# A streaming-encoder block on one core: q, the probabilities and the attention output turned by VectorE and GpSimd, none by TensorE

## The reference

```python
x = x + 0.5 * swiglu(rms_norm(x, norm_ffn1_w), ffn1_w_gate, ffn1_w_up, ffn1_w_down)      # width 5632
p = rms_norm(x, norm_mix_w) @ w_in                                                        # width 5376
# group A: 16 query heads of 64 over 2 key heads, chunks of 64 tokens; a chunk sees itself and the one before
logits = einsum('bnqhgd,bnkhd->bnhgqk', qc, kb) * 64 ** -0.5      # -inf where there is no chunk before
probs = softmax(concatenate([logits, sink], axis=-1))[..., :-1]
attn_out = einsum('bnhgqk,bnkhd->bnqhgd', probs, vb)
# group B: retention, 4 heads of 256: rotary(q), rotary(k), decay, group norm, swish gate
x = x + concatenate([attn_out, ret_out]) @ w_out
x = x + 0.5 * swiglu(rms_norm(x, norm_ffn2_w), ffn2_w_gate, ffn2_w_up, ffn2_w_down)
out = rms_norm(x, norm_final_w)
```

## Time and profile before

| | |
|---|---|
| median of 3 runs | 1823.14 us (1823.1 to 1823.24) |
| profiled execution | 1823.17 us, its span 1821.4 us |
| TensorE | 1807.5 us busy, 99% |
| VectorE | 1183.8 us busy, 65% |
| ScalarE | 823.5 us busy, 45% |
| GpSimd | 63.6 us busy, 3% |
| DMA, mean rate | 190 GB/s |

### The profile page before, as it was taken

How to read it: one execution, slowest core, us unless ns; L and a number is a source line. 1 busy time by engine, 2 the same in 40 slices (tenths; PEclk the granted TensorE clock), 3 DMA queues, 4 the chain that set the end, 5 groups by cost and what they waited for, 6 DMA issues and landing times.

```text
span 1821.4 us, 22695 instructions
## 1 busy us (share of the span) xinstructions
PE 1807.5 (99%) x8314; PEld 1495.8 (82%) x8314; DVE 1183.8 (65%) x1399; ACT 823.5 (45%) x986; POOL 63.6 (3%) x59
## 2 busy tenths in 40 slices
PE   9999999999999999999999999999999999999998
PEld 6888888888888888888888888888888888888886
DVE  5666676676676667544466665676676666667666
ACT  6434444443443445455555455444443443444444
POOL 0000000000000000100045000000000000000000
PEclk9999999999999999999999999999999999999999
DMA  9565565655556555555545456556556556555562
GB/s 371 194 199 185 197 194 187 199 189 191 201 185 196 195 186 187 182 167 179 163 160 185 139 176 208 194 186 203 187 191 201 185 195 197 186 199 191 189 204 93
DMA packets 175235, 346.64 MB, mean 190 GB/s; under 512 B 5984, under 2 KB 8416, under 8 KB 175072
## 3 DMA queue, kind: packets, MB, share of 16 engines
q1 hardware_dynamic: 174768, 345.61, 57.3%
q10 hardware_dynamic: 432, 0.55, 0.1%
HBM read 344.04 MB, written 2.10 MB: 190 GB/s over the span
## 4 chain that ended last, share of the span: by engine, by line
PE 98%; DVE 1%; DMA 1%; issue 0%; ACT 0%; SPq 0%; POOLq 0%; POOL 0%; DVEq 0%
PE ps L328 32%; PE ps L330 32%; PE ps L329 32%; PE ps L355 1%; DMA raw<-in_g 1%; DVE w_lo L850 0%; PE ps L475 0%; PE ps L563 0%; PE ps L574 0%; PE ps L488 0%; ACT w_hi L638 0%; PE ps L444 0%; PE ps L442 0%; PE ps L443 0%; DVE x L914 0%
## 5 line engine op out<-in xcount | busy, mean ns | idle before, releaser
L850 DVE TENSOR_TENSOR w_lo<-raw,w_hi 128x1024 fp32r<-128x1024 f32 x648 | 806.0, 1245 | 603.6 <-ACT w_hi L638 602.5
L638 ACT ACTIVATE w_hi<-raw 128x1024 fp32r<-128x1024 f32 x648 | 687.0, 1061 | 966.9 <-PE ps L330 957.1
L328 PE MATMUL ps<-w_hi,xT_hi 128*128 128x512 f32 (+1 forms) x1816 | 706.7, 389 | 1.7 <-DVE w_lo L850 1.1
L329 PE MATMUL ps<-w_lo,xT_hi 128*128 128x512 f32 (+1 forms) x1816 | 703.4, 387 | 0.0
L330 PE MATMUL ps<-w_hi,xT_lo 128*128 128x512 f32 (+1 forms) x1816 | 703.4, 387 | 0.0
L328 PEld LDWEIGHTS ps<-w_hi,xT_hi 128*128 128x128 f32 x1816 | 341.0, 188 | 72.5 <-DVE w_lo L850 1.6
L330 PEld LDWEIGHTS ps<-w_hi,xT_lo 128*128 128x128 f32 x1816 | 341.0, 188 | 70.1
L329 PEld LDWEIGHTS ps<-w_lo,xT_hi 128*128 128x128 f32 x1816 | 341.0, 188 | 68.7
L328 PE MATMUL ps<-w_hi,hT_hi 128*128 128x512 f32 x640 | 249.1, 389 | 0.0
L330 PE MATMUL ps<-w_hi,hT_lo 128*128 128x512 f32 x640 | 249.0, 389 | 0.0
L329 PE MATMUL ps<-w_lo,hT_hi 128*128 128x512 f32 x640 | 249.0, 389 | 0.0
(11 more groups left out here) (110 smaller groups left out, 499.2 us busy)
## 6 DMA issues: line engine op xcount, KB each, us to landing
raw<-in_u SPq DMA_DIRECT2D x88, 1024.0 KB, 5.1
raw<-in_d SPq DMA_DIRECT2D x88, 1024.0 KB, 4.9
raw<-in_g SPq DMA_DIRECT2D x87, 1024.0 KB, 5.1
raw<-in_w_in SPq DMA_DIRECT2D x40, 1024.0 KB, 4.9
raw<-in_w_out SPq DMA_DIRECT2D x16, 1024.0 KB, 5.0
x<-in_x SPq DMA_DIRECT2D x4, 512.0 KB, 12.6
raw<-in_w_in SPq DMA_DIRECT2D x4, 512.0 KB, 3.6
out<-proj SPq DMA_DIRECT2D x8, 256.0 KB, 2.4
```

The source lines that it names most:

```text
L328: pe.matmul(out, xh, wh, start=first and j == 0, stop=False)
L329: pe.matmul(out, xh, wl, start=False, stop=False)
L638: act.activation(dst, raw[:, s, (k % 2) * HALF:(k % 2 + 1) * HALF], ACT.Copy).then_inc(hi_ready, 1)
L850: dve.tensor_tensor(w_lo[:, k % LEAD, :, :].rearrange(flat), raw[:, k // 2, (k % 2) * HALF:(k % 2 + 1) * HALF], f32(w_hi[:, k % LEAD, :, : ...
```

## The change

No block of q, probabilities or attention output goes through TensorE any more. VectorE turns a whole tile at once, but each 32 by 32 square where it stands (`dve.transpose` from SBUF to SBUF), and GpSimd copies the squares to the partitions where they belong: 8 copies for q, 16 for the probabilities, 16 for the attention output, each of 32 partitions. The results lie in `qT`, `probsT` and `attT_raw` (in `qT_full`) in SBUF. `q_in` and `att` become the two halves of one tile, `stage_tile`; the turned probabilities are put over both. `weigh` moves from behind half 10 to behind half 11, the division from VectorE's position 10 to 12, `attT_hi` and `attT_lo` from 13 to 15. GpSimd's loop over quads is written out. The core of the diff, with the waits:

```diff
@@ tensor
             def weigh(quad):
-                pe.wait_ge(probsT_a, quad)
-                pe.wait_ge(probsT_b, quad)
+                pe.wait_ge(probsT_ready, quad)
                 pe.wait_ge(v_in_ready, quad)
...
-                            if quad is not None and (e, k) == (0, 1):
-                                pe.wait_ge(kT_ready, 3)
-                                pe.wait_ge(q_in_ready, quad)
-                                for t in range(T):
-                                    for hh in range(QUAD):
-                                        mm = turn(B_DOWN + t, hh * P, q_in[:, t, hh * HD:(hh + 1) * HD])
-                                mm.then_inc(q_turned, 1)
                             if quad is not None and (e, k) == (0, 3):
                                 logits(quad)
-                            if quad is not None and (e, k) == (1, 0):
-                                pe.wait_ge(probs_ready, quad)
...
-                            if quad is not None and (e, k) == (1, 2):
+                            if quad is not None and (e, k) == (1, 3):
                                 weigh(quad)
-                            if quad is not None and (e, k) == (1, 5):
-                                pe.wait_ge(att_ready, quad)
...
@@ scalar
-                    if k == 1:
-                        act.wait_ge(q_turned, j + 1)
...
-                    if k == 13:
-                        act.wait_ge(att_turned, j + 1)
...
+                    if k == 15:
+                        act.wait_ge(attT_raw_ready, j + 1)
+                        act.activation(attT_hi[:, bass.ds(2 * j, 2), :], attT_raw, ACT.Copy).then_inc(attT_hi_ready, 1)
@@ vector
+                    if k == 0:
+                        dve.wait_ge(q_in_ready, j + 1)
+                        dve.transpose(q_blocks, q_in).then_inc(q_blocks_ready, 1)
...
+                    if k == 7:
+                        dve.wait_ge(probs_ready, j + 1)
+                        dve.transpose(probs_blocks, probs[:].rearrange("p t h c -> p (t h c)")
+                                      ).then_inc(probs_blocks_ready, 1)
...
+                        dve.wait_ge(att_ready, j + 1)
+                        dve.transpose(att_blocks, att).then_inc(att_blocks_ready, 1)
@@ gpsimd
+            def squares_of(size):
+                return [(d, c) for d in range(size // SQ) for c in range(P // SQ)]
+
+            def move_q(j):
+                pool.wait_ge(q_blocks_ready, j + 1)
+                pool.wait_ge(attT_lo_ready, j + 1)
+                pool.wait_ge(kT_in_ready, j + 1)
+                pool.wait_ge(v_in_ready, j + 1)
+                for d, c in squares_of(HD):
+                    to = qT_full[d * SQ:(d + 1) * SQ, :, :].rearrange("p t (h c) -> p t h c", h=QUAD)
+                    of = q_blocks[c * SQ:(c + 1) * SQ, :, :].rearrange("p t (h c) -> p t h c", h=QUAD)
+                    m = pool.tensor_copy(to[:, :, :, c * SQ:(c + 1) * SQ], of[:, :, :, d * SQ:(d + 1) * SQ])
+                m.then_inc(qT_ready, 1)
...
+            for j in range(NQ):
+                stage_kv(j)
+                move_q(j)
+                move_probs(j)
+                if j + 1 < NQ:
+                    stage_q(j + 1)
+                move_att(j)
+            pool.wait_ge(attT_lo_ready, 1 + NQ)
             pool.wait_ge(proj_ready, 2 + 7)
```

More of the change, by code:

```diff
@@ L126, in build @@
             h = sb("h", [P, T, W], F32, ffn)
-        q_in = sb("q_in", [P, T, QUAD * HD])
+        stage_tile = sb("stage_tile", [P, 2, T, QUAD * HD])
+        q_in, att = stage_tile[:, 0, :, :], stage_tile[:, 1, :, :]
         qT_full = sb("qT", [P, T, QUAD * P])
@@ L192, in build @@
         v_in_ready = sem("v_in_ready")
-        q_turned = sem("q_turned")
+        q_blocks_ready = sem("q_blocks_ready")
+        probs_blocks_ready = sem("probs_blocks_ready")
+        att_blocks_ready = sem("att_blocks_ready")
+        attT_raw_ready = sem("attT_raw_ready")
+        probsT_ready = sem("probsT_ready")
         qT_ready = sem("qT_ready")
@@ L1113, in rsqrt_of_norm, with stage_q @@
                                    ALU.pow).then_inc(rstd_ready, 1)
[L1115 to L1123, removed]
-                    pool.wait_ge(logits_ready, j)
[L1125 to L1130, removed]
-                    pool.wait_ge(pv_done, j)
-                pool.wait_ge(kT_in_ready, j + 1)
-                pool.tensor_copy(v[:], v_all[:, bass.ds(j // 2, 1), :, :, :].rearrange(
-                    "p g t v c -> p (g t) v c")).then_inc(v_in_ready, 1)
+            def stage_q(j):
+                pool.wait_ge(proj_ready, j + (2 + 1))
+                if j:
+                    pool.wait_ge(probsT_ready, j)
+                pool.tensor_copy(q_in, proj[:, :, A_Q + j * QUAD * HD:A_Q + (j + 1) * QUAD * HD]
+                                 ).then_inc(q_in_ready, 1)
@@ new lines, in move_probs @@
+            def move_probs(j):
+                pool.wait_ge(probs_blocks_ready, j + 1)
+                for d, c in squares_of(P):
+                    to = probsT[d * SQ:(d + 1) * SQ, :, :].rearrange("p t (h c) -> p t h c", h=QUAD)
+                    of = probs_blocks[c * SQ:(c + 1) * SQ, :].rearrange("p (t h c) -> p t h c", t=T, h=QUAD)
+                    m = pool.tensor_copy(to[:, :, :, c * SQ:(c + 1) * SQ], of[:, :, :, d * SQ:(d + 1) * SQ])
+                m.then_inc(probsT_ready, 1)
@@ new lines, in move_att @@
+            def move_att(j):
+                pool.wait_ge(att_blocks_ready, j + 1)
+                if j + 1 < NQ:
+                    pool.wait_ge(q_in_ready, j + 2)
+                for d, c in squares_of(P):
+                    to = attT_raw[d * SQ:(d + 1) * SQ, :, :].rearrange("p k (t c) -> p t k c", t=T)
+                    of = att_blocks[c * SQ:(c + 1) * SQ, :, :].rearrange("p t (k c) -> p t k c", k=2)
+                    m = pool.tensor_copy(to[:, :, :, c * SQ:(c + 1) * SQ], of[:, :, :, d * SQ:(d + 1) * SQ])
+                m.then_inc(attT_raw_ready, 1)
@@ L1176, in _ @@
             pool.wait_ge(v_ready, 4)
[L1177 to L1180, removed]
+            stage_q(0)
+            for j in range(NQ):
+                stage_kv(j)
+                move_q(j)
+                move_probs(j)
+                if j + 1 < NQ:
+                    stage_q(j + 1)
+                move_att(j)
+            pool.wait_ge(attT_lo_ready, 1 + NQ)
             pool.wait_ge(proj_ready, 2 + 7)
```

43 lines of the change are left out of this document (15 added, 28 removed).

## The result

The changed kernel takes 1883.49 us (median of 4 runs, 1882.46 to 1884.3) against 1823.19 us (1823.1 to 1823.41) for the kernel before: 1.0331 times as long, interval 1.0319 to 1.0343. That is slower, as forecast, but by 60.3 us where 26.7 were forecast, and outside the stated range of 1825 to 1876.

The account below looks back on a forecast made before the run. The prediction took TensorE to bound the kernel: 1823.2 us less 8.7 for removed turns, plus waits of 11.6 for the probabilities, 9.8 for q and 14 for the rotation, gave 1850 us, range 1825 to 1876.

Parts of the forecast that it names:

- What bounds the kernel: Whole kernel: TensorE, busy 99% of the span; time it is relieved of is won in full, waits lost in full.
- What is removed: TensorE's turns of q, probabilities and attention output: 2.18 us a quad, 8.7 us saved over four quads.
- the clock: Rival, chance 0.07: TensorE's clock falls to 1.2 GHz in nine new waits and one half after each, adding 24.6: 1874 us.
- The price of a copy: GpSimd's block copies: 0.30 us for 256 elements (bounds 0.26 and 0.40), 0.20 for 128 (0.16 and 0.29), fitting between VectorE's splits.
- The probabilities: Before weigh: copies held up by splits make TensorE wait 2.9 us a quad, 11.6 us in all.
- q: Before the logits: TensorE waits 1.4 us in the first quad, 2.8 in each of three later ones, 9.8 in all.
- e15: The time at which half 15 of a pair ends; the output's copies were forecast to end 3.0 us after it.
- e0: The time at which half 0 of a pair ends; q's turn was forecast to end 5.3 us after it, its copies 11.4.
- The rotation behind the last quad: After the last pair: the rotation starts later, delaying head 0's root; TensorE waits 14 us (bounds 3.7 and 17.7).
- Cheap copies: Rival, chance 0.18: GpSimd's copies overlap or cost well under 0.2 us, so q and probabilities are in time: 1828 us.
- faster: Rival, chance 0.05: copies are cheap and the rotation meets no split either, so it costs 3.7 us: 1818 us.
- Dear copies: Rival, chance 0.12: each GpSimd copy costs 0.61 us, as much as one of 512 elements, lengthening the waits: about 1880 us.

Follow-up runs that it names:

- f2: Changed kernel with q, weigh, division, attT, rotation and roots reordered, and the bank wait before half 3 put on the division: 1812.78 us, 0.9943 of the kernel before.
- e1: Changed kernel with TensorE kept busy by unused junk products ahead of the logits, weigh and the turn of head 0's output: 1863.9 us, ratio 1.0225.
- e2: Changed kernel with GpSimd's reciprocal root of each head put behind the next head's rotation instead of behind all four: 1869.12 us, ratio 1.025.
- e4: Changed kernel with the probabilities alone turned by TensorE again, behind half 8: 1868.56 us, ratio 1.0248.
- e3: As a run: changed kernel with q alone turned by TensorE again, 1859.91 us, ratio 1.0202. In "e3 = 845.93": the time at which half 3 ends.
- e5: Changed kernel with the attention output alone turned by TensorE again, behind half 14: 1875.16 us, ratio 1.0283.

## Why the prediction was right or wrong

- **What bounds the kernel** (each microsecond of TensorE won or lost in full): right. f2 shows the gain, the other runs the losses, and nothing on another engine mattered until TensorE waited for it.
- **What is removed**, 8.7: measured 9.2.
- **The step that failed is the clock.** I took the earlier trace rows (full clock in a window with 0.17 us busy of 2) and "no row has a longer pause" as evidence that nothing happens after a pause, gave it a chance of 0.07, and treated it as a rival. But a row near the start says nothing of waits of 2.7 to 4.6 us inside the dense stream, and the clock excludes none of the waits that I forecast: it is a term of the sum that they bring with them. Its size I had worked out nearly right (24.6 us, nine times one half of 2.73). Measured are 19.6 by e1, 18.8 by e2 to e4, and 25.3 by the busy times of the changed kernel and f2, which make the same 8234 matmuls (1824.4 less 1799.1). That the total fits is in part luck: behind the single waits 1.5 to 4.4 us were lost, and a tenth wait, at a half, lost some too. The Trainium skill, "TensorE: Matmul & The Clock Gate", section "What's actually happening", has an idle array throttled: the traces agree, with 0.50 to 0.52 behind the waits and 1.00 in e1.
- **The price of a copy**: 0.30 us taken with 0.40 as the upper bound, 0.20 and 0.29 for 128 elements. Measured from start to start are 0.44 and 0.33, both above my bounds. The bounds were durations; no part of a copy hides under the one before, which I had carried over from the rotations.
- **The probabilities**: the turn ends about when forecast, but four copies fit between splits and not five, so that `weigh` waits 3.5 us a quad, 14.2 against 11.6. This lies inside the bounds given for that wait (0.9 to 4.3).
- **q**: 16.4 against 9.8, the largest error among the waits. The chain was the one described, with each link later. The logits are due at e3 = 845.93, so e15 is 10.92 earlier, 835.01. The output's copies end at 838.90 (830.73 plus 8.17), which is e15+3.9 and not 3.0, and `attT_hi` and `attT_lo` are late with them; the turn ends at 843.92, which is e0+6.2 and not 5.3; no copy fits before split 1, and the last ends at e0+12.6 and not 11.4. I had counted 3.2 and then written 2.8, a step in the wrong direction with no row behind it. e5 shows the link: without the output's copies each wait is 2.7. The first quad's was forecast at 1.4 and was 2.7, by the price of the copy.
- **The rotation behind the last quad**: right. 14 forecast, 12.1 at the turn of head 0 measured. It lasts 43.1 us (1021.69 to 1064.79) where 41 were forecast, and e2 shows the cause, the root that stands behind all 24 operations. The 2.3 us more that TensorE waits at the halves are not of this term and were not forecast at all: the longest, 2.2, stands behind the late `attT_lo`, and in e5, without the output's copies, no wait there is over 0.6.
- **Cheap copies** and **faster**: refuted by the row of 64 copies and by the queue of held ones. **Dear copies** (0.61 us each) too: 0.44.

The account: 60.3 is 16.4 for q, 14.2 for the probabilities and 12.1 for the root, 2.3 at the halves, less 9.2, which is 35.8, and 24.5 remain. That is the clock: the busy times give 25.3 for it and the windows 25.6. e1 gains less, 21.6 in the profiled executions, for two reasons that its trace shows: its fillers and idle time are 1.3 longer than the idle time they stand for, and its other matmuls still take 2.4 more than f2's (1838.5 less 37.0 against 1799.1).

Set against the forecast of 26.7, the 33.6 us that are missing are 24.5 of clock, 6.6 for q, 2.6 for the probabilities and 2.3 at the halves, less 1.9 at the root and 0.5 at the turns. With the clock alone the forecast would have been about 1874, just inside the range; the waits together, those for q above all, took the time out of it.

It was not tried whether copies of more partitions at once would have been cheaper.

## What to carry to other kernels

Price a wait of the tensor engine as the idle time plus the slow stretch behind it; it belongs to the sum, not among the rivals, and a stretch of low activity at the kernel's start is no evidence for one in its middle. Work moved to slow side engines costs nothing if its result is asked for late enough, so before judging such a change by its copies, count how many of them fit between the collisions of one work step and put the consumer behind that; here `weigh` two halves later, q one quad ahead, and the rotation and roots moved turned +60 into -10 us. When a producer is moved, look for every wait that used it as a stand-in for something else: `attT_lo_ready` guarded PSUM banks, and leaving it there cost 17 us.

## What the runs showed of the hardware

GpSimd's copies of 32 partitions cost what those of 64 do, 0.40 us for 256 elements and 0.29 for 128, and they run one after the other, 0.44 and 0.33 us from start to start. `memset` of the same places took 0.305 us and none of 64 was held by a split, while copies took up to 1.37. The clock fell to half behind waits of 2.7 to 4.6 us in the middle of dense work, and was 1.00 behind a pause of 2.25 us near the start of the kernel before (6.16 to 8.42 us; the windows of 2 us at 6 and at 8 show it). What was lost behind a wait was 3.1 to 4.4 us at q, 1.5 to 1.7 at `weigh` and 2.4 behind the 12.1 us; the length of the wait does not order them.
